# The forgetting heads' key bias inside the score product, and two inner chunks turned by VectorE instead of TensorE

## The reference

```python
s = jnp.einsum('bqhd,bshd->bhqs', q_blk, k).astype(jnp.float32) * (HEAD_DIM ** -0.5)
s = s + jnp.transpose(cum_blk, (0, 2, 1))[..., None] - jnp.transpose(cum, (0, 2, 1))[:, :, None, :]
p = jax.nn.softmax(jnp.where(dist >= 0, s, -jnp.inf), axis=-1)
```

```python
h = rms_norm(x, mlp_norm_g[l])
x = x + jnp.square(jax.nn.relu(h @ w_up[l])) @ w_down[l]
```

## Time and profile before

| | |
|---|---|
| median of 3 runs | 780.82 us (780.65 to 780.98) |
| span of the profiled execution | 778.9 us, granted clock 1.000 |
| PE busy | 766.9 us, 98% |
| DVE busy | 585.3 us, 75% |
| ACT busy | 408.0 us, 52% |
| POOL busy | 47.5 us, 6% |

### The profile page before, as it was taken

The page is one execution under the profiler, slowest core; times in us unless marked ns, Lnnn a source line. Parts: engine busy times, 40 slices in busy tenths (PEclk is TensorE's granted clock), DMA queues, the critical chain, the costliest instruction groups (busy, mean ns, idle before and its releaser), DMA issues.

```text
span 778.9 us, 9688 instructions
## 1 busy us (share of the span) xinstructions
PE 766.9 (98%) x3758; PEld 642.5 (82%) x3758; DVE 585.3 (75%) x925; ACT 408.0 (52%) x547; POOL 47.5 (6%) x38
## 2 busy tenths in 40 slices
PE   7999999999999999999999999999999999999998
PEld 5878889888888888888888887888988888888886
DVE  5689687796766878687888748699857778668585
ACT  6555455455556736555545555764555354343431
POOL 1100000000001410000000004132000000000000
PEclk9999999999999999999999999999999999999999
DMA  9943424344454455656555663945123665656511
GB/s 340 334 161 94 153 84 163 136 151 151 156 163 161 163 199 198 218 182 212 195 185 170 208 216 133 353 158 175 55 94 124 215 210 173 212 170 208 196 74 55
DMA packets 67453, 136.25 MB, mean 175 GB/s; under 512 B 2384, under 2 KB 5072, under 8 KB 66768
## 3 DMA queue, kind: packets, MB, share of 16 engines
q1 hardware_dynamic: 67120, 134.52, 50.5%
q10 hardware_dynamic: 288, 1.12, 0.4%
HBM read 134.43 MB, written 1.05 MB: 174 GB/s over the span
## 4 chain that ended last, share of the span: by engine, by line
PE 90%; DVE 7%; ACT 2%; issue 1%; DMA 0%; DVEq 0%; ACTq 0%
PE b L630 20%; PE b L632 20%; PE b L631 20%; PE SS L630 4%; PE SS L632 4%; PE SS L631 4%; PE TT L599 3%; PE OO L630 2%; PE OO L632 2%; PE OO L631 2%; DVE wlo L1571 1%; PE OO L946 1%; DVE ca L2085 1%; PE b L775 1%; PE SS L718 1%
## 5 line engine op out<-in xcount | busy, mean ns | idle before, releaser
L1571 DVE TENSOR_TENSOR wlo<-raw,whi 128x2048 fp32r<-128x2048 f32 (+2 forms) x121 | 274.5, 2270 | 82.5 <-ACT whi L1109 81.7
L1109 ACT CAST whi<-raw 128x2048 fp32r<-128x2048 f32 (+2 forms) x121 | 227.1, 1878 | 135.8 <-PE b L632 94.6
L630 PE MATMUL b<-whi,Ahi 128*128 128x512 f32 (+2 forms) x536 | 213.7, 399 | 2.7 <-DVE Alo L1594 1.6
L632 PE MATMUL b<-whi,Alo 128*128 128x512 f32 (+2 forms) x536 | 206.5, 385 | 0.0
L631 PE MATMUL b<-wlo,Ahi 128*128 128x512 f32 (+2 forms) x536 | 206.0, 384 | 0.0
L630 PEld LDWEIGHTS b<-whi,Ahi 128*128 128x128 f32 x536 | 101.2, 189 | 22.5 <-DVE Alo L1594 2.4
L632 PEld LDWEIGHTS b<-whi,Alo 128*128 128x128 f32 x536 | 101.0, 189 | 20.9
L631 PEld LDWEIGHTS b<-wlo,Ahi 128*128 128x128 f32 x536 | 101.4, 189 | 18.2
L1959 DVE STREAM_TRANSPOSE hT<-ust 32x256 f32<-32x256 f32 (+1 forms) x192 | 81.5, 425 | 2.7
L630 PE MATMUL b<-whi,Bhi 128*128 128x512 f32 x154 | 60.4, 392 | 0.0
L632 PE MATMUL b<-whi,Blo 128*128 128x512 f32 x154 | 60.0, 389 | 0.0
(11 more groups left out here) (285 smaller groups left out, 1078.3 us busy)
## 6 DMA issues: line engine op xcount, KB each, us to landing
raw<-in_w_in SPq DMA_DIRECT2D x40, 1024.0 KB, 4.9
raw<-in_w_up SPq DMA_DIRECT2D x16, 1024.0 KB, 5.4
raw<-in_w_dn SPq DMA_DIRECT2D x16, 1024.0 KB, 5.0
raw<-in_w_d SPq DMA_DIRECT2D x11, 1024.0 KB, 4.9
raw<-in_w_g SPq DMA_DIRECT2D x10, 1024.0 KB, 5.0
raw<-in_w_u SPq DMA_DIRECT2D x10, 1024.0 KB, 5.1
raw<-in_w_out SPq DMA_DIRECT2D x8, 1024.0 KB, 5.0
raw<-in_w_br SPq DMA_DIRECT2D x4, 1024.0 KB, 5.0
```

Source lines behind the costliest of these rows:

```text
L630: e.matmul(dst, xh, H[:, kc, c0:ce], start=first and kc == krs[0], stop=False)
L632: ins = e.matmul(dst, xl, H[:, kc, c0:ce], start=False, stop=last and kc == krs[-1])
L1109: e.copy(whi[:, s, 0:m], raw[:, r, 0:m]).then_inc(s_hi, 1)
L1571: e.tensor_tensor(wlo[:, s, 0:m], raw[:, r, 0:m], whi[:, s, 0:m].bitcast(F32), ALU.subtract).then_inc(s_lo, 1)
```

## The change

**Key bias.** The product that adds the bias goes, with `nl` and its semaphore. Instead `fm` writes the negative log gates of the four heads into columns 0, 32, 64 and 96 of a zeroed `nlf`; `fc` multiplies it once by the triangle, which gives the four heads' running sums over all 256 keys in rows 0, 32, 64, 96 of a bank; `fq` copies each as one row into the key tile of its head, in a row that belongs to the other half. The query tiles get ones in that row (POOL). Since both heads of a key tile need such a row, the even heads' keys go to tiles 6 and 10 (used before by dilated heads 0 and 1), which the new function `fox_k` knows. New waits: `fq` and the keys' turning wait for dilated task 3, POOL for the stick-breaking scores.

**Inner chunks.** `HV`, the list of chunks that DVE turns, gets chunks 0 and 7. Chunk 0: its parts stand in up 1 (part 0 in group 0, parts 1 and 2 in group 1, part 3 in group 2), and its high split moves from group 1 to group 2. Chunk 7: parts 0 and 1 stand in group 1 of down 6, parts 2 and 3 in group 2, and its high split moves from group 2 to group 3. The transposes on PE go.

```diff
-        if kind == "fox" and q == 0:
-            bg[a - 1].append(("nl", h))
...
-    HV = {("H", j): i for i, j in enumerate(range(1, 7))}
-    HV.update({("G", j): 6 + i for i, j in enumerate(range(6))})
+    HV = {("H", j): j for j in range(8)}
+    HV.update({("G", j): 8 + j for j in range(6)})
...
+    def fox_k(h):
+        return qkA[:, 8 + h // 2 if h % 2 else 6 + 4 * (h // 2), :]
...
                 w.wait_ge(s_fq, 1)
-                w.wait_ge(s_nl, h + 1)
+                w.wait_ge(s_one, 2)
...
-                e.matmul(Z[:, 0:m], qkA[:, 2 * a + pr, qs], qkA[:, 8 + pr, 0:m], start=True, stop=False)
-                ins = e.matmul(Z[:, 0:m], nlf[:, 0, :], c1("UO", 0, m), start=False, stop=qb == 0)
-                if qb:
-                    ins = e.matmul(Z[:, 128:256], nlf[:, 1, :], c1("UO", 0, 128), start=False, stop=True)
-                ins.then_inc(s_z, 1)
+                e.matmul(Z[:, 0:m], qkA[:, 2 * a + pr, qs], fox_k(h)[:, 0:m], start=True, stop=True).then_inc(s_z, 1)
...
-            e.matmul(o1, c1("UO", 0, 128), lf[:, 4:8], start=False, stop=True).then_inc(s_fc, 1)
+            e.matmul(o1, c1("UO", 0, 128), lf[:, 4:8], start=False, stop=True)
+            R = bank[bk][:, 128:384]
+            e.matmul(R, nlf[:, 0, :], c1("UO", 0, 256), start=True, stop=False)
+            e.matmul(R[:, 128:256], nlf[:, 1, :], c1("UO", 0, 128), start=False, stop=True).then_inc(s_fc, 1)
...
-                up("up", j, "N1", Bhi, Blo, (lambda q: last_h() if q == 1 else None) if j == 1 else None)
...
-                down("dn", j - 1, "H", False, (lambda k: turn_h() if k == 2 else None) if j == 7 else None)
+                down("dn", j - 1, "H", False)
...
-                if j and q == 1:
+                if j and q == (2 if j == 1 else 1):
                     hidden_hi(j - 1)
...
-                    if j == 7 and k == 2:
+                    if j == 7 and k == 3:
                         hidden_hi(7)
...
+            if dst == 18:
+                w.wait_ge(s_z, 4)
...
-            if dst in KTILE:
+            if dst == 18 and m < 2:
+                tile = qkA[row, 6:11:4, :]
+            elif dst in KTILE:
...
+            l4 = lf.rearrange("p (t h) -> p t h", t=2)
+            n4 = nlf[:].rearrange("p t (i x) -> p t i x", i=4)
+            e.tensor_scalar(n4[:, :, 0:2, 0], l4[:, :, 1:4:2], -1.0, None, ALU.mult)
+            e.tensor_scalar(n4[:, :, 2:4, 0], l4[:, :, 0:3:2], -1.0, None, ALU.mult).then_inc(s_fm, 1)
...
-            e.tensor_copy(cumq[:, 4:8], bk[:, 64:68]).then_inc(s_fq, 1)
+            e.tensor_copy(cumq[:, 4:8], bk[:, 64:68])
+            w.wait_ge(s_sz, 4)
+            w.wait_ge(s_z, 4)
+            for i, h in enumerate((1, 3, 0, 2)):
+                r = 0 if h % 2 else 64
+                ins = e.tensor_copy(fox_k(h)[r:r + 1, :], bk[32 * i:32 * i + 1, 128:384])
+            ins.then_inc(s_fq, 1)
...
                 before("up", j, ui, t)
-                if ("H", j - 1) in HV and q == 0:
+                if j == 1 and q < 3:
+                    for m in ((0,), (1, 2), (3,))[q]:
+                        turn_part(("H", 0), m, (s_up, 2))
+                if j > 1 and q == 0:
                     turn_part(("H", j - 1), 3, (s_up, 2 * j))
                 if j and q == 2:
                     hidden_lo(j - 1)
...
                     before("dn", j - 1, n, t)
-                    if ("H", j) in HV and k:
+                    if j < 7 and k:
                         turn_part(("H", j), k - 1, (s_up, 2 * j + 2))
+                    if j == 7 and k in (1, 2):
+                        turn_part(("H", 7), 2 * k - 2, (s_up, 16))
+                        turn_part(("H", 7), 2 * k - 1, (s_up, 16))
                     if j == 7 and k == 3:
                         hidden_lo(7)
...
+        e.memset(nlf[:], 0.0).then_inc(s_nz, 1)
+        w.wait_ge(s_sz, 4)
+        w.wait_ge(s_nz, 1)
+        e.memset(qkA[64:65, 0:2, :], 1.0).then_inc(s_one, 1)
+        w.wait_ge(s_one, 1)
+        e.memset(qkA[0:1, 2:4, :], 1.0).then_inc(s_one, 1)
```

More of the change, by code:

```diff
@@ L138, in timetable1 @@
         bg[71].append(("tu", 2 + t))
-    rank = {"wr": 0, "so": 0, "fq": 0, "nl": 0, "vt": 2}
+    rank = {"wr": 0, "so": 0, "fq": 0, "vt": 2}
     for s in bg:
@@ L277, in build @@
         sem(n) for n in ("s_flogit", "s_pair_dve", "s_sb_mask", "s_sb_soft", "s_sb_sub", "s_sb_out")]
-    s_zf, s_m, s_cb, s_w, s_fm, s_fq, s_nl = [
-        sem(n) for n in ("s_bias", "s_max", "s_combine", "s_write", "s_fmin", "s_fcum", "s_nlf")]
+    s_zf, s_m, s_cb, s_w, s_fm, s_fq = [
+        sem(n) for n in ("s_bias", "s_max", "s_combine", "s_write", "s_fmin", "s_fcum")]
+    s_one, s_nz = sem("s_ones_rows"), sem("s_nlf_zero")
     s_dn, s_gm, s_mix, s_res, s_rr, s_ra = [
@@ L905, in _ @@
         for j in range(8):
[L906 to L913, removed]
-                up("up", j, "N1", Bhi, Blo, (lambda q: last_h() if q == 1 else None) if j == 1 else None)
-            last_h = turn_h
+            up("up", j, "N1", Bhi, Blo, (lambda q: turn_res("N1", 1, 1) if q == 0 else None) if j == 0 else None)
             gone[1], gone[2] = (s_up, 2 * j + 1), (s_up, 2 * j + 2)
             if j:
-                down("dn", j - 1, "H", False, (lambda k: turn_h() if k == 2 else None) if j == 7 else None)
+                down("dn", j - 1, "H", False)
         down("dn", 7, "H", True, lambda k: k and turn_res("N2", *ORD[k - 1]))
@@ L1778, in fm @@
             w.wait_ge(s_fl, 1)
-            e.scalar_tensor_tensor(out=lf, in0=ff, scalar=0.0, in1=e1, op0=ALU.min, op1=ALU.subtract).then_inc(s_fm, 1)
+            k = own(e.scalar_tensor_tensor(out=lf, in0=ff, scalar=0.0, in1=e1, op0=ALU.min, op1=ALU.subtract))
+            w.wait_ge(s_dve, k)
+            w.wait_ge(s_nz, 1)
[3 more added lines that the diff above has]
+            e.tensor_scalar(n4[:, :, 2:4, 0], l4[:, :, 0:3:2], -1.0, None, ALU.mult).then_inc(s_fm, 1)
         def fq():
@@ L1838, in stages1 @@
                     fq()
-                elif name == "nl":
-                    nl(i)
                 elif name == "dn":
```

## The result

The changed kernel takes 784.85 us in the median (784.21 to 785.05, 4 runs), the kernel before 780.90 beside it (780.65 to 781.66): ratio 1.0047, interval 1.0035 to 1.0060. It is slower, by 3.95 us. The profiled execution took 784.21 us; its span is 782.2 us, against 778.9 before, and its granted clock 0.998, against 1.000.

A forecast was written before the change was run, and what follows sets the result against it. PE's instruction stream was taken as the bound. From 780.82, -3.15 for the bias, +0.75 for chunk 0 and +4.0 for chunk 7 gave 782.4, stated as 782.5 us; range 779.8 to 785.3.

The forecast's parts named there:

- A: Whole kernel: both PE stalls at the chunks as worked out, clock unchanged, 782.5 us, own range 781.6 to 783.3; chance 0.48.
- rival B: Behind chunk 7's wait: PE falls to 1.2 GHz, losing 1.6 to 3.3 us more; 784.1 to 785.8, middle 784.9; chance 0.22.
- The bias part: Key bias in the forgetting heads: products removed, new ones added, a wait gone; -3.15 us, between -2.3 and -3.2.
- the 0.65 of `fc`: Sum task of the key bias: one added product of 256 columns and one of 128, 0.43 + 0.22 = 0.65 us on PE.
- the 0.3 of the wait that went: PE before the first forgetting task: without the `nl` fill, DVE frees the score bank sooner; 0.32 us gained, lower bound 0.
- The four copies: DVE in `fq`: four copies of one partition x 256 from PSUM, taken as 1.4 us, between 0.6 and 1.9.
- rival E: Bias part's new chain: slow one-partition copies or a late evacuation, so it brings -1.6 instead of -3.15; 784.0 us; chance 0.08.
- Chunk 0: First down group: DVE turns the chunk late, PE waits 1.65 us against 0.87 of transposes saved; +0.75 us.
- Chunk 7: Before down 7: PE waits 4.9 us for the low half behind DVE's transposes and splits; +4.0 us against before.
- Its share of 2.2 us for the split: DVE before down 7: 2.2 of PE's 4.9 us wait are the weight split standing ahead of the low half.
- Nothing gives it back: PE behind the chunks: later steps are spaced by PE itself and splits can't run ahead, so no lost time returns.
- The clock: PE's clock behind the long wait: likeliest forecast left it unchanged, chance 0.48; a fall to 1.2 GHz had 0.22.

The follow-up runs named there:

- run 1: The change's key bias part alone, both chunks turned by PE as in the kernel before: 778.32 us, -3.2 against the kernel before, ratio 0.9955.
- run 4: The changed kernel with chunk 7's low half ahead of the weight split of group 3 on DVE: 782.81 us, ratio 1.0022 to the kernel before.
- run 6: The kernel before with chunks 0 and 7 turned by DVE as in the change, bias products as before: 787.82 us, ratio 1.0081 to the kernel before.
- run 3: The changed kernel plus ten unused PE products of 256 columns ahead of down 7: 784.01 us, ratio 1.0032 to the kernel before.

## Why the prediction was right, and where not

The sign and the place were right, and the time lay in the range; the likeliest case (A, 782.5) was not what came, rival B was (784.1 to 785.8).

- **The bias part, -3.15**: measured -3.2 in time (run 1), and -3.0 to -3.3 in the traces (-3.28 in the changed kernel at the first differential product; in run 1 -3.11 there and -3.03 at the last matmul). The products, the 0.65 of `fc` (124.45 to 125.11 in the timeline) and the 0.3 of the wait that went are all there. The Trainium skill (SBUF — State Buffer, "SBUF: two separate sides") says which DVE operations the lock of the shared port blocks, and a step with one SBUF input and one in PSUM isn't among them; the trace agrees, with 1.08 us for that step beside the fill.
- **The four copies, 1.4 us**: 1.71, near the upper bound of 1.9, with 0.4 us of slack left for the evacuation instead of 0.9. The later bias step that rival E feared is there, and by that slack it cost nothing.
- **Chunk 0, +0.75**: +0.78 at down 0, and 0.13 more behind it for the first matmul after the wait. PE was to start at 322.4 in the times of the kernel before, which is 319.2 with the bias part's gain taken off, and it did at 319.21. The prediction's own terms give 1.6 and 0.73 where it says 1.65 and 0.75 (9.51 us of DVE work went in as 9.55), which changes nothing. A wait of 1.49 was read where 1.65 were said: the trace counts from the modelled end of the last matmul, 0.16 us behind the place where the next would have begun.
- **Chunk 7, +4.0**: +3.97, the wait 4.72 where 4.9 were said, for the same reason. Its share of 2.2 us for the split was too large: run 4 took the split away and down 7 began 1.5 us earlier, since the cast then lay open.
- **Nothing gives it back**: 0.02 us over the last 306.
- **The clock**: this is the step that failed. A fall was given 0.22, the unchanged clock more than twice that, on the strength of the 2.3 us of silence at the end with the clock at 1.00. That row said nothing of 4.9 us, and the prediction had noted as much. The price in rival B, 1.6 to 3.3 us, was right at its lower end: 1.60 and 1.78 in two profiles of the changed kernel. That the time, 784.85, fell on rival B's middle of 784.9 is luck: that middle has the clock at some 2.4 us, and the timed difference, +3.95, is 0.7 more than the trace's +3.2. The profiled execution was the shortest of the four, and no run shows what else the 0.7 are. Every profile with a wait of 3.2 us or more at the inner chunks shows the low clock, four of four (changed kernel twice, runs 4 and 6), and the eight runs of the changed kernel list 0.998 or 0.996. So the case should have been the likelier one. The Trainium skill (TensorE: Matmul & The Clock Gate, "Part 1: The HAM clock gate (the "warmup" mystery)") has the clock throttled by default and after idling, which spoke for it, and the runs agree: 0.50 granted behind the wait, and 1.00 when the same wait was filled.

## What to carry to other kernels

Where PE is busy for 98%, handing its small work to an engine with 25% of idle time wins only if the work fits ahead of PE's next need in that engine's own order; so walk that order instruction by instruction, with its splits and casts, as two neighbouring rows of another chunk allow. A wait of some microseconds on PE is to be priced with the low clock that can follow, 1.6 us here behind waits of 3.2 and 4.7 us. When a hand-off comes late, look for an earlier half of the data: the same turning in smaller pieces, begun where the engine sat idle, gained 0.9 us at chunk 7 (10.88 from down 6 to down 7, against 11.79 before) where the change lost 3.97 + 1.60.

## What the runs showed of the hardware beyond that

- In the profiles a PE wait of 1.5 us left the clock at 2.4 GHz, and behind one of 3.2 and three of 4.7 us it stood at 1.2 GHz. With the wait of 3.2 us it fell after PE had gone back to work, and two of that kernel's eleven runs list no fall (1.000).
- The stretch behind the wait, 5.44 us in the kernel before, took 1.6 to 1.8 us more in each of the four (7.04, 7.22, 7.17 and 7.09 in the changed kernel twice and runs 4 and 6). Of that some 0.13 us are the first matmul after a wait: run 3, which kept the clock, took 5.57.
- A DVE copy from PSUM of 1 x 256 takes 0.43 us, close to the 0.41 estimated above for 128 x 256 and to the 0.47 of another 128 x 256 step alone. So one partition seems no shorter than 128, though the same operation wasn't run at both.
- A DVE transpose of 32 x 128 takes 0.31 us against 0.45 for 32 x 256, so turning in halves costs 40% more DVE time (10.1 us a chunk against 7.2).
